# A hybrid retention / delta-rule / expert-retrieval layer on one core: the first chunk's exponentials, output projection and first expert head in another order

## The reference, cut to what matters

```python
h = _rmsnorm(x, ln1_w)
rq, rk, rv, rg, gq, gk, gv, gz, ga, gb = split(h @ w_in)
y_r = groupnorm(retention(rope(rq), rope(rk), rv)) * ret_norm_w * silu(rg)
cq, ck, cv = split(silu(causal_short_conv([gq, gk, gv], conv_w)))
g = -exp(A_log) * softplus(ga + dt_bias);  beta = sigmoid(gb)
# chunk of the delta rule: decays exp(gc_i - gc_j), a triangular inverse of 128 x 128 per head
y_g = rmsnorm(gated_delta_rule(l2(cq), l2(ck), cv, g, beta)) * silu(gz)
x = x + concat(y_r, y_g) @ w_out
h2 = _rmsnorm(x, ln2_w)
q = (h2 @ wq).reshape(128, 8, 2, 128); s = einsum('thpd,hpkd->thpk', q, sub_keys)
ids, gate = top-16 of the 256 sums of the top-16 of each half, softmax     # 8 heads x 16 = 128 slots
x = x + sum_slots gate * gelu(u_tab[ids] . h2) * v_tab[ids]
return _rmsnorm(x, lnf_w)
```

## Time and profile before

| what | value |
|---|---|
| three runs | 3212.75, 3224.86, 3225.95 us; median 3224.86 |
| the profiled execution | 3213.71 us, its span 3211.9 us |
| busy share of the span | PE 75%, DVE 64%, ACT 37%, POOL 35% |
| mean transfer rate | 394 GB/s over the span |

### The profile page before, as it was taken

One profiled execution on the slowest core, in us unless ns is written; L12 is line 12 of the kernel. 1 busy time (PEld: TensorE's weight loads), 2 busy tenths in 40 slices (PEclk: granted clock), 3 DMA queues, 4 the chain that ended last, 5 costly groups with the idle time before them and its releaser, 6 DMA issues.

```text
span 3211.9 us, 36177 instructions
## 1 busy us (share of the span) xinstructions
PE 2421.8 (75%) x12528; PEld 1407.8 (44%) x12528; DVE 2066.2 (64%) x5346; ACT 1176.7 (37%) x3387; POOL 1134.4 (35%) x1030
## 2 busy tenths in 40 slices
PE   7878678996885678997776677898778567765555
PEld 6764256762461245663453134674345124521111
DVE  4265764667658874667748884566856986486444
ACT  2132533344333532435332533335433343233222
POOL 0033332234324443334433343333433343344442
PEclk9888799998897899998988799998898688877777
DMA  8279989999999999999999999999999999999998
GB/s 332 72 303 414 402 307 400 368 419 420 385 402 414 421 413 417 407 421 421 421 403 399 421 421 409 420 418 421 421 411 389 421 421 413 421 397 422 422 421 337
DMA packets 176439, 1266.29 MB, mean 394 GB/s; under 512 B 20096, under 2 KB 20096, under 8 KB 23808
## 3 DMA queue, kind: packets, MB, share of 16 engines
q0 software_dynamic: 147456, 1073.81, 81.4%
q1 hardware_dynamic: 26928, 183.84, 14.0%
q10 hardware_dynamic: 1872, 6.33, 0.5%
HBM read 1259.71 MB, written 4.19 MB: 394 GB/s over the span
## 4 chain that ended last, share of the span: by engine, by line
PE 42%; DMA 30%; DVE 18%; ACT 8%; issue 2%; POOL 1%; ACTq 0%; POOLq 0%; DVEq 0%
DMA uv<-uv_tab,ids 23%; PE y_ps L445 14%; PE bank L502 12%; DVE uv L1022 9%; PE bank L494 8%; DMA wbuf<-w 6%; PE bank L509 2%; ACT diag L752 2%; PE y_ps L524 1%; PE bank L702 1%; DVE area L1279 1%; DVE area L1073 1%; ACT actT L780 1%; PE bank L537 1%; POOL uv L420 1%
## 5 line engine op out<-in xcount | busy, mean ns | idle before, releaser
L420 POOL DMA_INDIRECT uv<-uv_tab,ids x1024 | 1133.9, 1107 | 2047.7 <-PE y_ps L445 1689.3
L1022 DVE CUSTOM_DVE_ANT_0 uv<-uv,h 128x1024 f32<-128x1024 f32 x1024 | 1231.5, 1223 | 723.2 <-DMA uv<-uv_tab,ids 718.3
L445 PE MATMUL y_ps<-uv,diag 128*64 128x512 f32 x4096 | 1203.1, 720 | 549.9 <-ACT diag L752 527.5
L445 PEld LDWEIGHTS y_ps<-uv,diag 128*64 128x64 f32 x4096 | 291.3, 157 | 1225.7 <-ACT diag L752 750.2
L746 ACT ACTIVATE gelu<-dots 128x2 f32<-128x2 f32 x512 | 103.5, 202 | 1279.0 <-DVE dots L1022 1278.3
L502 PE MATMUL bank<-actT,wbuf 128*128 128x128 f32 x2688 | 352.8, 295 | 61.4 <-DMA wbuf<-w 46.6
L502 PEld LDWEIGHTS bank<-actT,wbuf 128*128 128x128 f32 x2688 | 339.2, 209 | 113.6 <-issue 65.3
L752 ACT ACTIVATE diag<-gated,gelu 128x64 f32<-128x64 f32 x1024 | 300.7, 340 | 59.0 <-ACT gelu L746 0.8
L742 ACT ACTIVATE gated<-smalls,gate 128x64 f32<-128x64 f32 x1024 | 293.7, 335 | 7.8 <-DVE acc L1036 7.8
L494 PE MATMUL bank<-wbuf,actT 128*128 128x256 f32 x960 | 227.6, 391 | 19.9 <-DMA wbuf<-w 17.1
L494 PEld LDWEIGHTS bank<-wbuf,actT 128*128 128x128 f32 x960 | 181.7, 194 | 89.8 <-issue 41.3
(11 more groups left out here) (212 smaller groups left out, 1918.9 us busy)
## 6 DMA issues: line engine op xcount, KB each, us to landing
wbuf<-w SPq DMA_DIRECT2D x146, 1024.0 KB, 9.5
uv<-w SPq DMA_DIRECT2D x20, 1024.0 KB, 18.4
uv<-uv_tab,ids POOLq DMA_INDIRECT x1024, 13.9
acc<-x SPq DMA_DIRECT2D x8, 512.0 KB, 12.4
y<-acc ACTq DMA_DIRECT2D x8, 512.0 KB, 7.9
rowbuf<-x SPq DMA_DIRECT2D x5, 512.0 KB, 11.4
actT_ahead<-x SPq DMA_DIRECT2D x3, 512.0 KB, 15.7
keys_sb<-keysT ACTq DMA_DIRECT2D x1, 1024.0 KB, 17.0
```

The costliest lines, as they stand in the source:

```text
L420: nc.gpsimd.indirect_dma_start(out=uv[i % RING][:, :, :].rearrange("p z d -> p (z d)"), out_offset=None, in_=uv_tab, in_offset=bass.Indire ...
L445: done = mm(y_ps[z][64 * j:64 * j + 64, :], diag[:, i % DIAGS, :], uv[i % RING][:, 1, 512 * z:512 * z + 512], start=(s % PAIRS == 0), stop ...
L1022: V.tensor_tensor_reduce(out=u, in0=u, in1=h2[n % 2][:, j, :], scale=1.0, scalar=0.0, op0=ALU.mult, op1=ALU.add, accum_out=dots[:, i % DOT ...
```

## The change

It touches the first chunk almost alone; two tables (`PIECES` and the place of the retention steps among the levels) act in all eight.

- PE makes the keys' projection ahead of the gate product; ACT makes the gate exponentials (`softplus`) right after the first conv input. DVE makes the log decays ahead of the third convolution, ACT the decays ahead of its silu.
- The retention rotations move between the levels, and every retention step one level later.
- `FILL` spreads 80 entries over 19 turns, up to the 23rd (before: 64 over 12, up to the 16th). The 16 new entries are the first half of the output projection: the retention half of its input is transposed as soon as it is there (into `actT_ahead`), and all four output blocks accumulate over it in `y_ps`; the second half follows when the delta rule's output is ready.
- Head 0 is chosen alone: a query block for it alone (`q0a`), its scores, 8 steps. Then head 1, 2-3, 4-7. The step windows: chunk 0 gets (-3, 20) in place of (-8, 24), so 28 steps, not 24, lie in the mixer of chunk 1. Steps now stand between the query products of chunk 0.

```diff
-GROUPS = [[(0, 2), (2, 4), (4, PH)] if n == 0 else [(0, 4), (4, PH)] for n in range(NCH)]
+GROUPS = [[(0, 1), (1, 2), (2, 4), (4, PH)] if n == 0 else [(0, 4), (4, PH)] for n in range(NCH)]
...
-FILL = {4: 10, 5: 4, 7: 10, 8: 8, 9: 4, 10: 4, 11: 4, 12: 4, 13: 4, 14: 4, 15: 4, 16: 4}
+FILL = {4: 4, 5: 2, 7: 8, 8: 2, **{mark: 4 for mark in range(9, 21)}, 21: 3, 22: 3, 23: 10}
...
-PIECES = ([2, 2.3, 1.7, 1, 1.6, 1.2, 2, 1.5]
-          + [1.2, 0.8, 0.7, 0.8, 1.3, 0.8, 1.2, 0.8, 0.7, 0.8, 0.5, 0.8] + [0.6, 0.8, 1.4, 0.6]
+PIECES = ([2, 2.3, 1.7, 1, 1.6, 1.2, 2, 0.5]
+          + [1.5, 0.8, 1.2, 0.8, 0.7, 0.8, 1.3, 0.8, 1.2, 0.8, 0.5, 0.8] + [0.7, 0.8, 1.4, 0.6]
...
-        return ((-8, 24), (48, 76))[n]
+        return ((-3, 20), (48, 76))[n]
...
                 if s == 0:
-                    pe.wait_ge(*event("gR_in", 0))
-                    pe.wait_ge(*event("gG_in", 0))
+                    pe.wait_ge(*event("x2", 0, 1))
...
+                blocks = []
+                for i in range(4):
+                    if i % 2 == 0:
+                        pe.wait_ge(*event(LATE_EVENTS[2 + i // 2], 0))
+                    if i == 0:
+                        pe.wait_ge(*event("mT", 0, 0))
+                    blocks.append(weight_block())
+                    for k in range(KT // 2):
+                        out_product(blocks, i, k)
+                        yield
+                pe.wait_ge(*event("mT", 0, 1))
+                for i in range(4):
+                    for k in range(KT // 2, KT):
+                        last = out_product(blocks, i, k)
+                        if k == KT - 1:
+                            last.then_inc(late_made if i % 2 else w_free, 1)
+                        yield
...
-                between = {1: ret_transposes, 2: ret_scores, 3: ret_out}
+                between = {2: ret_transposes, 3: ret_scores, 4: ret_out}
...
-                    project(n, "q0", cols_product, [actT], turn)
-                    sub_scores(n, (0,))
-                    turn()
-                    turn()
+                    given(cols_product(take(n, "q0a"), 0, weight_block(), actT))
+                    pe.wait_ge(*event("first_q", n))
+                    scores_of(n, "s0a", (0, 1))
+                    for _ in range(4):
+                        turn()
...
+            def rest_of_queries(at):
+                given(cols_product(take(0, "q0b"), 0, weight_block(), actT))
+                pe.wait_ge(*event("qT", 0, 0))
+                scores_of(0, "s0b", (2, 3))
+                replicate(0)
+                for j, f in ((1, 0.2), (2, 0.3), (3, 0.35)):
+                    project(0, f"q{j}", cols_product, [actT], nothing)
+                    sub_scores(0, (j,))
+                    at(f)
...
-                    inputs(Chunk(1), lambda f: at(0.25 + 0.75 * f))
+                    inputs(Chunk(1), lambda f: at(0.15 + 0.85 * f))
...
-                waiting = [(0.40, 0), (0.90, 1)] if n > 0 else [(0.45, 1), (0.90, 2)] if n == 0 else []
+                waiting = [(0.40, 0), (0.90, 1)] if n > 0 else [(0.22, 1), (0.45, 2), (0.90, 3)] if n == 0 else []
...
-                between = {1: ret_queries, 2: ret_decay_scores, 3: ret_moments, 4: ret_group_norm, 5: gate_weight}
+                between = {1: ret_rotations, 2: ret_queries, 3: ret_decay_scores, 4: ret_moments, 5: ret_group_norm}
```

More of the change, by code:

```diff
@@ L121, in last_fills @@
         if kind == "start":
-            places += [None if name in LATE_NAMES else PLACE[n, name] for name in IN_NAMES]
-        elif kind != "second":
+            places += [None if name in LATE_NAMES else PLACE[n, name] for name in IN_NAMES] + [None, None]
+            places += [PLACE[n, name] for name in ("q0b", "q1", "q2", "q3")]
+            continue
+        if kind != "second":
             places += [PLACE[n, name + "+" * (kind == "first")] for name in IN_NAMES]
@@ L306, in build @@
         }
-        for _, e, m, _, _ in USES["alone"]:
+        for _, e, m, _, _ in USES["start"] + USES["alone"]:
             per_chunk[e] = m
@@ L528, in late_products, with out_product, scores_of @@
                             yield
-            late = late_products()
+                blocks = []
[15 more added lines that the diff above has]
+                        yield
+            def out_product(blocks, i, k):
+                return mm(y_ps[i // 2][:, WB * (i % 2):WB * (i % 2) + WB], actT_ahead[:, k, :], blocks[i][:, k, :],
+                          start=(k == 0 and i % 2 == 0), stop=(k == KT - 1), skip_group_check=True)
+            late = late_products()
+            def scores_of(n, name, tiles):
+                b = take(n, name)
+                for i, t in enumerate(tiles):
+                    last = mm(b[:, P * i:P * i + P], qT[:, t, :], keys_sb[:, t, :], start=True, stop=True)
+                given(last)
             def sub_scores(n, which):
@@ L534, in sub_scores @@
                     pe.wait_ge(*event("qT", n, j))
[L535 to L539, removed]
+                    scores_of(n, f"s{j}", range(4 * j, 4 * j + 4))
             def inputs(c, at):
@@ L559, in inputs @@
                     given(last)
+                at(0.25)
+                for a, src in zip(c.ahead, projected):
+                    pe.wait_ge(*event("hT", n + a, 1))
+                    if n > 0:
+                        gate_product(a, src)
                 products, done = 14 * len(projected), [0]
@@ L946, in mix, with two @@
                     put_scores(c, j)
+            def two(c, name, use, dst):
+                A(dst, heads(filled(act, use, c))[:, 0:2, :], ACT.Copy).then_inc(S[name], 1)
             def put_scores(c, j):
@@ L972, in route @@
                 if n == 0:
-                    for j in (1, 2, 3):
+                    two(c, "qT", "q0b", qT[:, 2:4, :])
+                    two(c, "scores", "s0b", scores[:, 2:4, :])
+                    gates(0, 0)
+                    replicated(c)
+                    for j, f in ((1, 0.2), (2, 0.3), (3, 0.35)):
                         put("qT", f"q{j}", qT[:, 4 * j:4 * j + 4, :], c)
                         put_scores(c, j)
-                        if j == 1:
-                            gates(0, 0)
-                            replicated(c)
+                        at(f)
                 elif n > 0:
```

207 lines of the change are left out of this document (131 added, 76 removed).

## The result

| | median of its runs | lowest to highest |
|---|---|---|
| before (4 runs, same chip) | 3223.32 us | 3212.75 to 3225.95 |
| after (4 runs) | 3246.34 us | 3238.85 to 3250.54 |

The ratio of after to before is 1.0075, 95% interval 1.0045 to 1.0105: the change makes the kernel 0.75% slower, little but clear of the noise. The profiled execution of after took 3238.85 us, its span is 25.1 us longer than that of before.

The account below looks back on a forecast made before the run. The prediction took the DMA engines as the bound, with gains only from their idle times: -20 for the earlier start and -8 in chunk 1's mixer, -28 on 3213.71, 3186 (3197 from the median); it said 3190, range 3172 to 3212.

Parts of the forecast that it names:

- Slower, by the moved pieces: Rival, chance 0.05: `PIECES` makes PE's steps late in all seven later mixers and empties the ring; 8 us each gives 3242.
- (a): Chunk 0, convolutions to the keys' product: earlier gate exponentials and fewer late fill matmuls, -9.4 us.
- (b): Chunk 0, keys' product to the first level: less fill and rotations moved away, -3.1 us; first level near 61.6.
- (c): Chunk 0, the six levels: the spread fill costs nothing, 0 us; 40.5 us before.
- (d): Chunk 0, from wT to the mixed rows' transposes: 13.0 us before, -1 us.
- (e): Chunk 0, output projection: half its matmuls left, transposes to x2 from 18.3 to 8.2 us, -10 us.
- (f): Chunk 0, norm and its transposes, 145.93 to 152.55 us before: unchanged.
- (g): Chunk 0, first query to the first MAX8: 32 instructions, not 64, from 12.2 to 7.6 us, -4.6 us.
- (h): Chunk 0, selection to the first gather: one head, not two, from 16.4 to 10.8 us, -5.6 us.
- Chunk 1's mixer: 370 to 500 us: four more steps there fill part of 18 us of idle DMA time, -8 us.
- the start: Chunk 0, to about 200 us: the earlier first gather's lead, 9.1 MB or 21.6 us of full rate, taken as 20 us.
- its rival: Chunk 0's query products, chance 0.14: PE waits for gathers, the ring eats the lead, 10 us are left: 3204.

Follow-up runs that it names:

- e1: The changed kernel with the old `PIECES` table for the mixers of chunks 2 to 7: 3194.02 us, ratio 0.9922 to before.
- e5: The changed kernel, new table kept, with turns' places half a step earlier in the 39-step mixers alone: 3187.91 us, ratio 0.9922 to before.
- e10: The kernel before, its own table kept, with places 0.4 of a step later in the four 39-step mixers: 3235.59 us, ratio 1.0054 to before.

## Why the prediction was wrong

**The step that failed** is the price of the moved table. The prediction counted it in chunk 1's mixer alone ("I cannot see where in the idle parts it lands"), took nothing for it after 600 us, and gave the rival *Slower, by the moved pieces* a twentieth, with the reason that the share of 1.00 "has 9 buffers, 22 us, of slack behind it". What the runs showed in its place: in the four 39-step mixers the table makes pairs of steps, the transfer share falls to 0.96 to 0.99 from 1000 to 2400 us, and with the old table there 49 us come back (e1). The prediction's own sign of being wrong, a share under 0.98 in a later mixer, came up. Two things were wrong in it.

First, the table was read as a list of shares, of which a few differ by half a step. What the engines see are whole steps per turn, and these can be worked out from the table without a run: the two rows of counts above. The rival looked for steps that come late; what cost were pairs, as e5 and e10 show.

Second, the slack. The 9 buffers are a stock against late data for DVE. For the DMA engines it is the gathers already issued and not yet landed that count: in before, from 1060 to 1260 us, the median gather lands 14.6 us after its issue, not 22, and DVE waits six times, up to 1.4 us, for one to land, so it uses some as soon as they are there. Two pairs in successive levels, with waits of POOL for buffers of 4.2 and 6.4 us, were enough to use that up. The loss is paid in one mixer after the other: 8, 6 and 6 gathers in the three windows counted. The rival's own price, 8 us at each of seven mixers for 3242, is near the 3246 measured, but by luck: it was meant for late steps in seven mixers, and the loss came from pairs in four at some 12 us each.

**The other steps**, on the chain that ended last in after. Start, duration, what:

```profile
42.62 2.49 PE bank L631 x16
...
59.19 1.16 PE bank L520 x8
...
101.12 0.89 PE bank L520 x8
...
113.46 0.45 PE bank L480 x4
...
114.58 7.19 PE y_ps L562 x32
...
121.80 0.70 DVE acc L1346
...
128.60 5.74 PE bank L513 x32
...
147.04 1.11 POOL uv L432
```

- (a) and (b): the sums start at 42.62 where the text had 44.7, the first level at 59.19 where it had 61.6. The gain to the first level is 14.9 us, not 12.5, and the difference lies in (a).
- (c) and (d): from the first level to the mixed rows' transposes 54.3 us; before it was 53.5. The text had 52.5. The six levels up to wT (101.12) take 41.9 us where 40.5 was taken, with 0.4 of it for the retention half's transposes; the rest, (d), takes 12.3 where 12.0 was taken.
- (e): transposes to x2 8.3 us (8.2 in the text), the second half 32 matmuls in 7.19 us (6.9).
- (f) and (g): 6.8 us to the first query, then 7.4 us to its first MAX8 (7.6 in the text; the MAX8 row is in the next fence).
- (h): 11.1 us to the first gather (10.8). The first gather goes at 147.04; the text had 148.

The timeline of after from the first scores to the ninth gather:

```profile
135.96 0.49 DVE L1383 MAX8 area<-arena 128x8 f32<-128x128 f32 x2 [11.77 <-ACT arena L1040]
...
152.72 1.23 DVE L1118 CUSTOM_DVE_ANT_0 uv<-uv,h 128x1024 f32<-128x1024 f32 x1 [5.44 <-DMA uv<-uv_tab,ids]
...
155.07 0.94 POOL L432 DMA_INDIRECT uv<-uv_tab,ids  x1 [0.30 <-issue]
...
159.14 3.68 PE L456 MATMUL y_ps<-uv,diag 128*64 128x512 f32 x8 [6.04 <-ACT diag L816]
...
180.17 0.94 POOL L432 DMA_INDIRECT uv<-uv_tab,ids  x1 [24.17 <-PE bank L513]
183.74 0.94 POOL L432 DMA_INDIRECT uv<-uv_tab,ids  x1 [2.63 <-PE bank L513]
```

Seven gathers, then the gap; the eighth at 180.17 (183 in the text), the ninth at 183.74 (187), 9.6 us ahead of before. The step between is there at 159, and PE waits 6.0 us for it (8 in the text). Chunk 1's mixer gained 0.07 x 130 = 9 us of share, where 8 were taken. What the text took for the start and that mixer together, 28 us, is close to what e1 gains, 3219.77 - 3194.02 = 25.8 us. That is in part luck, as the rates by stage show (GB/s, and the difference in MB and in us at 0.42 MB/us):

| stage, us | before | e1 | MB | us |
|---|---|---|---|---|
| 60 to 200 | 125 | 179 | +7.6 | +18 |
| 200 to 370 | 416 | 396 | -3.4 | -8 |
| 370 to 500 | 335 | 364 | +3.8 | +9 |
| 500 to 600 | 376 | 360 | -1.6 | -4 |
| 600 to 1000 | 406 | 413 | +2.8 | +7 |

The start and the mixer came about as taken (20 and 8), but the sum had neither the 12 us that the stages behind them give back nor the 7 us that chunk 2's stage gains. The prediction's high end also has a slip: with 10 us of lead left, as in its rival, the upper level of 3225 gives 3215, not 3212.

**Table loads.** After pays a switch of set for the last silu, and again the load lasts 1.28 us and the activation starts 1.29 us after the load's start:

```profile
48.11 1.28 ACT L938 ACT_TABLE_LOAD   x1
49.40 0.63 ACT L938 ACTIVATE area<-area 128x512 f32<-128x512 f32 x1
```

The Trainium skill, *ScalarE: Activation LUTs*, section "What ACT_TABLE_LOAD costs", has 2.66 us for it with the drain; this trace shows no drain between load and activation. The silu ended at 50.0 us, ahead of the 53.2 that the sum by the row had, with squares and sums earlier.

## What to carry to other kernels

Where a schedule scales a table of shares and then issues whole units, write out the whole numbers for every place that uses it before and after an edit, also where the edit isn't meant to act: 0.02 of a step decided over one of the pairs here. A full transfer share in a stretch says what bounds it, not how much its engines have in hand; look there at the time from issue to landing and at how long the consumer waits for data. Units that two engines hand to each other should come one by one: in the pair traced here PE waited 5.0 us for DVE and DVE 5.2 us for PE, and PE's clock was 0.50 after its wait.

## What the runs showed of the hardware that was not expected

- The first gather was in use 5.7 us after its issue (147.04 to 152.72), with nothing but gathers in the DMA queues, against the 8.9 us of before that the prediction carried over. In before two weight loads of 1 MB went beside them (27% of the engines' time from 174 to 191 us); that these are the reason is not tested.
- A wait of PE of 5 us inside a mixer was followed by a granted clock of 0.50, and a step of eight matmuls took 3.68 us instead of 1.94. Where PE is waited for, its wait so lengthens the work behind it.
